# Squares of the second norm added on VectorE, silus and sigmoids of the token mixing in pairs

## The chip, the core and the metric

The kernel runs on one core of one Trainium2 chip. The metric is the device time of one execution in microseconds (us). The engines of the core work side by side, each through its own list of instructions: TensorE (PE, matrix products; PEld is its weight load), VectorE (DVE), ScalarE (ACT), GpSimdE (POOL), and SyncE (SP), which only starts transfers here. They wait for one another on semaphores, counters that an instruction raises when it is done.

## What is computed

Two blocks of a language model in fp32, for one sequence of 256 tokens with 1024 channels. Only what bears on the change stands here:

```python
def reference(x, ...):
    x = first_block(x, ...)      # short convolution and gated delta rule, w_o, then a feed-forward net
    return second_block(x, ...)

def first_block(x, ...):
    ...
    x = x + conv_ffn(rmsnorm(x, norm_ffn_g), w_up, ffn_conv_w, w_down)
    return rmsnorm(x, norm_final_g)

def second_block(x, ...):
    xn = rmsnorm_2(x, norm1_g)
    qa, ka, va, qr, kr, vr, gr, gate_a, gate_b = [xn @ part for part in w_in]
    qa, ka = rmsnorm_2(qa per head, q_norm_g), rmsnorm_2(ka per head, k_norm_g)
    o_a = dilated attention of qa, ka, va
    o_r = head_groupnorm(retention(qr, kr, vr), ret_gn_g, ret_gn_b) * silu(gr)
    y = sigmoid(gate_a) * (o_a @ w_proj_a) + sigmoid(gate_b) * (o_r @ w_proj_b)
    x = x + y @ w_out
    return x + square(relu(rmsnorm_2(x, norm2_g) @ w_up)) @ w_down
```

The "second norm" of the title (norm 2 in the code, counted from 0) is the final norm of the first block and the first of the second block taken together: it needs two sums of squares over the channels, one of x and one of x times the gain `norm_final_g`.

## The kernel before

**Blocks.** All weights are cut into 177 blocks of 1 MB (16 tiles of 128 x 128). `plan()` lists them; a block has a kind and a number, as ("qa", 0), and `AT` gives its place n. TensorE goes through them in `stream(n)`. To keep fp32 accuracy with a faster matrix format, each factor is split in a high and a low part, and a tile product is three matmuls: high x high, high x low, low x high, 48 to a block. Activations stand transposed, channels on the partitions and the 256 tokens along them; a block mostly makes two channel tiles, a 128 x 512 result.

**The path of a weight block.** SyncE loads block n + 3 into one of four buffers (`raw`) once TensorE is done with block n - 1. ScalarE makes the high part `wh` (`split`, L898) and VectorE the low part `wl` = raw - wh (L1225, 128 x 2048). In step n each engine does the split of block n + 3, then what `schedule()` puts into `TODO[n]` with `put(n, step, ...)`, in the order of the puts. VectorE first evicts the result of block n out of PSUM (`take(n)`, times the norm's factor `rb`), then splits, then does its steps. Exceptions stand in tables: for n in `AHEAD` VectorE splits block n + 3 before the norm and the eviction; `LOW_LATE` and `HIGH_LATE` put the split behind the steps. TensorE has two PSUM banks for these results (psS0, psS1), so block n can begin once block n - 2 is evicted. What TODO[n - 1] gives TensorE is strewn into its stream of block n: a lone norm 2 after 5 of 16 tiles, a lone step after 8, two steps after 5 and 10.

**The second norm.** The last blocks of the first net are d1 8 to d1 10; behind them come qa 0, qa 1 and so on. `res2(j)` (VectorE, ScalarE) adds the residual to pair j of the channel tiles, for j = 0 to 3, and makes its high and low parts (Yh, Yl), which qa 0 reads. In `sum2(j)` ScalarE squares the pair into `sq` and, with the gain, into `t2` (two buffers each), and GpSimdE adds them onto `ss0` and `ss1` (`add_squares(2, j)`, `tt` at L1631). Tile pair 3 has the buffers of pair 1, so ScalarE's `squares` waits until the adds of pair 1 are done. `norm(2)`: TensorE sums ss0 and ss1 over the partitions (L577), ScalarE and VectorE make from it `rfin` and `rb`, and VectorE can evict qa 0. For each pair of heads `sqh` squares the evicted queries: ScalarE makes the high part of the square (Zh), GpSimdE the whole square `sq` and then the low part Zl = sq - Zh; in the next block TensorE sums both (`colsum2`, L624 and L625), and ScalarE and VectorE finish the head's norm (`rmsh`).

**The stretch gr to tb.** Blocks gr 0 to gr 7 are the retention's gate, ta 0 to 3 and tb 0 to 3 the two gates of the mixing. VectorE evicts each to `y[n % 2]`. ScalarE takes it from there through silu (`silur`, L986) or sigmoid (`sig`, L974). The next eviction to the same y has to wait for that:

```python
if before in SIG:                       # before = SEQ[n - 2]
    dve.wait_ge(sem["sg"], SIG[before] + 1)
if before and before[0] in ("z", "gr"):
    dve.wait_ge(sem["zs" if before[0] == "z" else "sr"], before[1] + 1)
tt(y[n % 2][:], ps, two(rb[:]), ALU.mult, "ev")
```

Beside these blocks runs the group norm of the retention, from gr 3 to tb 0, one piece i a step: `ret_o(i)` (TensorE's product, L850; VectorE's bn_stats, bn_aggr and, once ScalarE has made the inverse deviation with Ln and Exp at L1165 and L1167, the scaled result `acc`, L1563), `ret_t(i - 1)` (TensorE transposes it, L860; ScalarE scales it, L1175; GpSimdE multiplies by silu(gr)) and `ret_x(i - 2)` (high part L901 and low part). ScalarE holds one table of functions at a time: silu, sigmoid, and Ln with Exp each need another one, and ACT_TABLE_LOAD fetches it. Copy and Square work with each.

Of the kernel before, what the change touches and what calls it, by code (L numbers as in the profile page):

```python
# [16 lines left out]
ALU = mybir.AluOpType  # L17
# [49 lines left out]
AT = {key: n for n, key in enumerate(SEQ)}  # L67
# [60 lines left out]
def schedule():  # L128
# [3 lines left out]
    def put(n, step, *a):  # L132
        todo[n].append((step, a))
# [4 lines left out]
    for i, kind in enumerate("kqv"):  # L138
        for j in range(4):
            n = AT[(kind, j)]  # L140
# [12 lines left out]
    for h in range(0, H1, 2):  # L153
        n = 10 + h // 2
# [22 lines left out]
    for j in range(4):  # L177
        n = AT[("x", j)]
# [3 lines left out]
        n = AT[("gb", j)]  # L182
        put(n + 1, "sig", "gb", j)
    for j in range(4):
        n = AT[("z", j)]
# [5 lines left out]
    for j in range(FF1):  # L191
        n = AT[("u1", j)]
# [4 lines left out]
    for step, q, j in (("res2", 0, 8), ("sum2", 0, 8), ("res2", 1, 9), ("res2", 2, 10), ("wl", AT[("d1", 9)] + 3, 10),  # L197
                       ("sum2", 1, 10), ("sum2", 2, 10), ("res2", 3, 10), ("sum2", 3, 10)):
        put(AT[("d1", j)], step, q)
# [3 lines left out]
    for kind in ("qa", "ka"):  # L203
        for j in range(6):
            n = AT[(kind, j)]
# [4 lines left out]
    n = AT[("kr", 0)]  # L210
# [7 lines left out]
    n = AT[("vr", 2)]  # L218
    for h in range(RH):
        put(n + h, "ret_s", h)  # L220
    for i in range(8):
        put(AT[("gr", i)] + 1, "silur", i)
    n = AT[("gr", 3)]
# [7 lines left out]
    for kind in ("ta", "tb"):  # L231
        for j in range(4):
            put(AT[(kind, j)], "sig", kind, j)
    put(AT[("pa", 1)], "ma")
# [9 lines left out]


TODO = schedule()

LASTS = (AT[("wo", 3)], AT[("d1", 10)], AT[("w2", 3)])
AHEAD = {n + 1 for n in LASTS}

# [33 lines left out]
def program(nc, wts, par_d, x_d, abw_d, sums_d, mask_d, sel_d, md_d, dr_d, out_d):  # L284
    with ExitStack() as ctx:
# [3 lines left out]
        sem = {name: ctx.enter_context(nc.semaphore("s_" + name)) for name in SEMS}  # L289
# [586 lines left out]
        def _(act):  # L876
# [323 lines left out]
            for n in range(-1, NB):  # L1200
# [14 lines left out]
                for step, a in TODO[n]:  # L1215
                    if step in steps:
                        steps[step](*a)
# [5 lines left out]
        def _(dve):  # L1223
# [269 lines left out]
            def res2(j):  # L1493
# [5 lines left out]
                gained(Yl, Yh, lambda k: gg[:, k:k + 1], "xbh", "xb", j)  # L1499

            def res3(j):
                complete("w2", j)
                tt(pair(xT, j), psA[j][:], pair(xT, j), ALU.add, "r3")
                gained(Xl, Xh, lambda k: pcol("g_n2", k), "x3h", "x3", j)
# [81 lines left out]
            def res4(q):  # L1586
# [5 lines left out]
                     "rows": rows, "kk": kk, "tok": tok, "level": level, "state": state, "wstate": wstate,  # L1592
                     "onorm": onorm, "mixc": mixc, "mix": mix, "res1": res1, "res2": res2, "res3": res3, "x2": x2,
                     "rtok": rtok_, "rmsh": rmsh, "att_s": att_s_, "att_o": att_o, "ret_s": ret_s, "ret_o": ret_o,
# [34 lines left out]
        def _(pool):  # L1629
            def tt(out, a, b, op, name):  # L1630
                pool.tensor_tensor(out, a, b, op).then_inc(sem[name], 1)  # L1631
# [99 lines left out]
            def add_squares(i, j):  # L1731
                base = {1: 0, 2: 2, 3: 7}[i]
                per = 2 if i == 2 else 1
                done = {1: 0, 2: 4, 3: 12}[i]
                if j == 0:
                    return
                for g in range(per):
                    pool.wait_ge(sem["sqr"], done + per * j + g + 1)
                    src = (sq, t2)[g][j % 2][:]
                    last = j == 3 and g == per - 1  # L1740
                    name = "ss" if last else "ssa"
                    if j > 1:
                        pool.wait_ge(sem["ssa"], base + per * (j - 2) + g + 1)
                    tt(ss[g][:], ss[g][:], src, ALU.add, name)

# [12 lines left out]
            def ffn2(j):  # L1758
# [5 lines left out]
                     "lev0": lev0, "level": level, "state": state, "osq": osq, "sqh": sqh, "zg": zg, "mix": mix,  # L1764
                     "res1": lambda j: add_squares(1, j), "sum2": lambda j: add_squares(2, j),
                     "res3": lambda j: add_squares(3, j), "ret_t": ret_t,
# [97 lines left out]
```

## Time and profile before

| | us |
|---|---|
| median of 3 runs | 1154.15 |
| lowest, highest run | 1153.98, 1157.34 |
| the profiled execution | 1158.51 |
| its span, first to last instruction | 1156.7 |
| busy in the span: TensorE | 1137.4 |
| VectorE | 768.6 |
| ScalarE | 603.4 |
| GpSimdE | 206.2 |
| mean granted clock of TensorE, share of full | 0.997 |

The profile is a record of one execution. Times in it count from the start of the span. In a timeline a row is one instruction or several alike, and the bracket tells how long its engine had been idle and whose work ended that; with no bracket the engine had been busy. Instructions follow one another before the one ahead has wholly ended, so that two of 0.69 us may take 1.29 us together. Tile names are without buffer numbers: psS is psS0 or psS1, and mix or gdn are memory regions that hold many tiles in turn.

### The profile page before, as it was taken

The numbers are of one execution on the slowest core, as the hardware profiler recorded it, in microseconds if no ns is written. First come the engines' busy times: TensorE is split into PE (matmuls) and PEld (weight loads), VectorE is DVE, ScalarE is ACT, GpSimd is POOL, SyncE is SP. The second block draws the span as 40 slices with busy tenths as digits, with TensorE's granted clock in tenths as the row PEclk, the third lists the DMA queues.
The fourth block names the chain that finished last, engine by engine and source line by source line (L and its number), as shares of the span: only waits on it lengthen the run. The fifth ranks groups of instructions, "written<-read, shape, count | busy, mean of one in ns | idle before, by whom it ended". The sixth has DMA issues, their size and how long they took to land. (4 is left out here: it accounts for less than half of the span.)

```text
span 1156.7 us, 23245 instructions
## 1 busy us (share of the span) xinstructions
PE 1137.4 (98%) x10262; PEld 1103.4 (95%) x10262; DVE 768.6 (66%) x875; ACT 603.4 (52%) x692; POOL 206.2 (18%) x129
## 2 busy tenths in 40 slices
PE   8999999999999999999899999999999999999998
PEld 7978899999999999999899999999999999999998
DVE  7999775435456897796768757645666556756453
ACT  6978342242664765565655534433798335544341
POOL 0442353210133200000445400000011002211010
PEclk9999999999999999999999999999999999999999
DMA  8443332333365555655555553445445555556552
GB/s 306 149 142 127 137 111 80 106 110 132 124 222 202 194 185 187 208 190 187 178 178 168 169 187 133 146 146 182 146 146 166 191 190 182 183 187 206 191 187 105
DMA packets 27748, 192.81 MB, mean 167 GB/s; under 512 B 3072, under 2 KB 3200, under 8 KB 4992
## 3 DMA queue, kind: packets, MB, share of 16 engines
q1 hardware_dynamic: 27648, 191.33, 48.9%
q8 instruction: 81, 1.33, 0.5%
q14 instruction: 19, 0.16, 0.0%
HBM read 190.27 MB, written 1.05 MB: 165 GB/s over the span
## 5 line engine op out<-in xcount | busy, mean ns | idle before, releaser
L1225 DVE TENSOR_TENSOR wl<-raw,wh 128x2048 fp32r<-128x2048 f32 (+1 forms) x178 | 421.3, 2369 | 134.9 <-ACT wh L898 134.0
L898 ACT ACTIVATE wh<-raw 128x2048 fp32r<-128x2048 f32 x176 | 336.5, 1913 | 248.3 <-DMA raw<-in_wts 248.0
L563 PE MATMUL psS<-Yh,wh 128*128 128x256 f32 x1056 | 300.3, 284 | 1.4 <-issue 1.1
L563 PE MATMUL psS<-Yl,wh 128*128 128x256 f32 x1056 | 293.4, 278 | 0.0
L563 PE MATMUL psS<-Yh,wl 128*128 128x256 f32 x1056 | 293.4, 278 | 0.0
L563 PE MATMUL psS<-Xh,wh 128*128 128x256 f32 x896 | 260.7, 291 | 4.8 <-issue 3.2
L563 PE MATMUL psS<-Xl,wh 128*128 128x256 f32 x896 | 249.7, 279 | 0.0
L563 PE MATMUL psS<-Xh,wl 128*128 128x256 f32 x896 | 249.7, 279 | 0.0
L563 PEld LDWEIGHTS psS<-Yh,wh 128*128 128x128 f32 x1056 | 199.1, 189 | 4.5 <-issue 3.4
L563 PEld LDWEIGHTS psS<-Yl,wh 128*128 128x128 f32 x1056 | 198.9, 188 | 2.5 <-issue 1.9
L563 PEld LDWEIGHTS psS<-Yh,wl 128*128 128x128 f32 x1056 | 198.4, 188 | 0.0
L563 PEld LDWEIGHTS psS<-Xh,wh 128*128 128x128 f32 x896 | 168.7, 188 | 15.4 <-issue 11.0
L563 PEld LDWEIGHTS psS<-Xl,wh 128*128 128x128 f32 x896 | 169.6, 189 | 3.2 <-issue 3.2
L563 PEld LDWEIGHTS psS<-Xh,wl 128*128 128x128 f32 x896 | 169.0, 189 | 0.0
L1231 DVE SCALAR_TENSOR_TENSOR acc<-y,par,acc 128x254 f32<-128x254 f32 (+1 forms) x176 | 79.8, 517 | 8.1 <-ACT acc L946 8.1
L1225 DVE TENSOR_TENSOR y<-psS,rb 128x512 f32<-128x512 f32 x66 | 45.4, 688 | 47.8 <-PE psS L563 44.1
L1631 POOL TENSOR_TENSOR t<-t,mix 128x512 f32<-128x512 f32 x12 | 15.7, 1309 | 290.2 <-ACT t L1175 224.0
L551 PE MATMUL psS<-wh,Yh 128*128 128x256 f32 x224 | 63.4, 283 | 0.0
L551 PE MATMUL psS<-wh,Yl 128*128 128x256 f32 x224 | 62.4, 278 | 0.0
L551 PE MATMUL psS<-wl,Yh 128*128 128x256 f32 x224 | 62.3, 278 | 0.0
L1631 POOL TENSOR_TENSOR ss<-ss,sq 128x512 f32<-128x512 f32 x9 | 17.8, 1975 | 212.4 <-ACT sq L1099 212.4
L563 PE MATMUL psP<-Yh,wh 128*128 128x256 f32 x192 | 53.3, 278 | 0.0
(246 smaller groups left out, 2004.6 us busy)
## 6 DMA issues: line engine op xcount, KB each, us to landing
raw<-in_wts SPq DMA_DIRECT2D x176, 1024.0 KB, 4.9
raw<-in_wts SPq DMA_DIRECT2D x2, 512.0 KB, 5.8
gdn<-in_x SPq DMA_DIRECT2D x1, 1024.0 KB, 8.2
out<-head SPq DMA_DIRECT2D x4, 256.0 KB, 2.1
head<-in_x SPq DMA_DIRECT2D x1, 516.0 KB, 4.0
head<-in_x SPq DMA_DIRECT2D x1, 512.0 KB, 5.9
head<-in_sel SPq DMA_DIRECT2D x1, 512.0 KB, 4.8
xf<-in_dr SPq DMA_DIRECT2D x1, 512.0 KB, 5.6
```

The source lines that it names most:

```text
L551: mm = pe.matmul(o, a[:, kk_, t * P:(t + 1) * P], b, start=(p == 0 and t == 0 and i == 0), stop=(p == 14 and i == 2), skip_group_check=True)
L563: mm = pe.matmul(bank[:, half], a[:, n % SLOTS, p, :], b[:, kk_, :], start=(first and i == 0), stop=(last and i == 2), skip_group_check=True)
L898: act.activation(wh[:, n % SLOTS], raw[:, n % SLOTS], ACT.Copy).then_inc(sem["wh"], 1)
L1225: return dve.tensor_tensor(out, a, b, op)
L1231: dve.scalar_tensor_tensor(out=out, in0=a, scalar=s, in1=b, op0=op0, op1=op1).then_inc(sem[name], 1)
L1631: pool.tensor_tensor(out, a, b, op).then_inc(sem[name], 1)
```

## The change

The edits fall in two groups.

At the second norm: the adds of squares (`sum2`) go from GpSimdE to VectorE; for that, `res2(3)` stands before them in the schedule, and ScalarE keeps its old order by an exception (it squares pairs 1 and 2 before `res2(3)`). And qa 0 leaves `AHEAD`, so VectorE splits qa 3 after the eviction of qa 0 rather than before the norm.

In the stretch gr to tb: `silur` of two tiles stands in the step after the odd one, and `sig` of two ta tiles in the step of the odd one. The tb tiles stay as they were. TensorE's list of instructions is the same as before.

```diff
@@ schedule()
     for step, q, j in (("res2", 0, 8), ("sum2", 0, 8), ("res2", 1, 9), ("res2", 2, 10), ("wl", AT[("d1", 9)] + 3, 10),
-                       ("sum2", 1, 10), ("sum2", 2, 10), ("res2", 3, 10), ("sum2", 3, 10)):
+                       ("res2", 3, 10), ("sum2", 1, 10), ("sum2", 2, 10), ("sum2", 3, 10)):
...
     for i in range(8):
-        put(AT[("gr", i)] + 1, "silur", i)
+        put(AT[("gr", i | 1)] + 1, "silur", i)
...
         for j in range(4):
-            put(AT[(kind, j)], "sig", kind, j)
+            put(AT[(kind, j | 1 if kind == "ta" else j)], "sig", kind, j)
...
-AHEAD = {n + 1 for n in LASTS}
+AHEAD = {LASTS[0] + 1, LASTS[2] + 1}
@@ ScalarE
                 for step, a in TODO[n]:
-                    if step in steps:
+                    if step == "res2" and a == (3,):
+                        sum2(1)
+                        sum2(2)
+                    if step in steps and (step, a) not in (("sum2", (1,)), ("sum2", (2,))):
                         steps[step](*a)
@@ VectorE
+            def sum2(j):
+                if j == 0:
+                    return
+                for g in range(2):
+                    dve.wait_ge(sem["sqr"], 4 + 2 * j + g + 1)
+                    if j > 1:
+                        dve.wait_ge(sem["ssa"], 2 + 2 * (j - 2) + g + 1)
+                    tt(ss[g][:], ss[g][:], (sq, t2)[g][j % 2][:], ALU.add, "ss" if j == 3 and g else "ssa")
@@ GpSimdE
-                     "res1": lambda j: add_squares(1, j), "sum2": lambda j: add_squares(2, j),
+                     "res1": lambda j: add_squares(1, j),
```

VectorE around the second norm, before: the residual of pair 3, its low halves, the low parts of blocks qa 2 and qa 3, the norm, the evictions of qa 0 and qa 1, and the low part of qa 4.

```order
L1225 TENSOR_TENSOR head<-psP1,head 128x512 [waits s_mm]
L1231 SCALAR_TENSOR_TENSOR Yl<-head,small,Yh 128x256 [waits s_xbh] x2
L1225 TENSOR_TENSOR wl<-raw,wh 128x2048 [waits s_wh] x2
L1225 TENSOR_TENSOR lnt<-psP2,rfin 128x256 [waits s_nl]
L1225 TENSOR_TENSOR lnt<-lnt,rfin 128x256 [waits s_ms0]
L1225 TENSOR_TENSOR rb<-lnt,rfin 128x256 [waits s_nl]
L1225 TENSOR_TENSOR mix2<-psS0,rb 128x512 [waits s_rb,s_mm]
L1225 TENSOR_TENSOR mix2<-psS1,rb 128x512 [waits s_mm]
L1225 TENSOR_TENSOR wl<-raw,wh 128x2048 [waits s_wh]
```

After:

```order
L1228 TENSOR_TENSOR ss0<-ss0,sq1 128x512 [waits s_sqr]
L1228 TENSOR_TENSOR ss1<-ss1,t21 128x512 [waits s_sqr]
L1228 TENSOR_TENSOR ss0<-ss0,sq0 128x512 [waits s_ssa,s_sqr]
L1228 TENSOR_TENSOR ss1<-ss1,t20 128x512 [waits s_ssa,s_sqr]
L1228 TENSOR_TENSOR ss0<-ss0,sq1 128x512 [waits s_ssa,s_sqr]
L1228 TENSOR_TENSOR ss1<-ss1,t21 128x512 [waits s_ssa,s_sqr]
L1228 TENSOR_TENSOR wl<-raw,wh 128x2048 [waits s_wh]
L1228 TENSOR_TENSOR lnt<-psP2,rfin 128x256 [waits s_nl]
L1228 TENSOR_TENSOR lnt<-lnt,rfin 128x256 [waits s_ms0]
L1228 TENSOR_TENSOR rb<-lnt,rfin 128x256 [waits s_nl]
L1228 TENSOR_TENSOR mix2<-psS0,rb 128x512 [waits s_rb,s_mm]
L1228 TENSOR_TENSOR wl<-raw,wh 128x2048 [waits s_wh]
```

The six adds now stand between the low halves and the first wl, and of the two wl ahead of the norm the second now stands between the two evictions (mix2<-psS0 and mix2<-psS1).

ScalarE in the stretch, before: the steps of gr 5 and, from the second wh on, the start of gr 6. Each begins with the split (wh<-raw); mix2<-y is a silu, rsd the statistics, t20 and t21 the transposed result.

```order
L898 ACTIVATE wh<-raw 128x2048 [waits s_mm,s_raw3]
L986 ACT_TABLE_LOAD
L986 ACTIVATE mix2<-y1 128x512 [waits s_ev]
L882 ACT_TABLE_LOAD
L1165 ACTIVATE rsd<-bag,par 128x1 [waits s_bag]
L1167 ACTIVATE rsd<-rsd 128x1 [waits s_rl]
L901 ACTIVATE Zh<-t20 128x4x128 [waits s_rg]
L1175 ACTIVATE t21<-psP0,par 128x128 [waits s_qk,s_rtT]
L1175 ACTIVATE t21<-psP0,par 128x128 x3
L898 ACTIVATE wh<-raw 128x2048 [waits s_mm,s_raw0]
```

After, the steps of gr 5 and the start of gr 6:

```order
L898 ACTIVATE wh<-raw 128x2048 [waits s_mm,s_raw3]
L1165 ACTIVATE rsd<-bag,par 128x1 [waits s_bag]
L1167 ACTIVATE rsd<-rsd 128x1 [waits s_rl]
L901 ACTIVATE Zh<-t20 128x4x128 [waits s_rg]
L1175 ACTIVATE t21<-psP0,par 128x128 [waits s_qk,s_rtT]
L1175 ACTIVATE t21<-psP0,par 128x128 x3
L898 ACTIVATE wh<-raw 128x2048 [waits s_mm,s_raw0]
L986 ACT_TABLE_LOAD
L986 ACTIVATE mix2<-y1 128x512 [waits s_ev]
L986 ACTIVATE mix2<-y0 128x512 [waits s_ev]
L882 ACT_TABLE_LOAD
```

In gr 5 both table loads and the silu are gone, and gr 6 has two silus between two loads; the second of them is the one that stood at this place before, the first (of gr 4) is new in this step. VectorE's list in this stretch is unchanged: an eviction, a wl, the statistics.

## Rows read from the trace of the kernel before

**Rows 1.** The page, part 1: engines, busy us (share of the span) xinstructions
```profile
PE 1137.4 (98%) x10262; PEld 1103.4 (95%) x10262; DVE 768.6 (66%) x875; ACT 603.4 (52%) x692; POOL 206.2 (18%) x129
```

**Rows 2.** Timeline, TensorE: start us, us, operation, [idle before <-releaser]
```profile
574.73 3.52 PE L577 MATMUL psP<-ss,par 128*128 128x256 f32 x8 [3.02 <-POOL ss L1631]
...
582.48 0.36 PE L563 MATMUL psS<-Yh,wh 128*128 128x256 f32 x1 [0.46 <-issue]
...
585.12 0.48 PE L624 MATMUL psP<-Zh,onesr 128*128 128x512 f32 x1 [0.68 <-POOL Zl L1631]
...
878.01 0.66 PE L860 MATMUL psP<-par,acc 128*128 128x128 f32 x4 [0.54 <-DVE acc L1563]
...
887.52 0.36 PE L563 MATMUL psS<-Yh,wh 128*128 128x256 f32 x1 [0.68 <-issue]
```

**Rows 3.** Windows of TensorE: stretch, us, busy (x), granted clock, DMA share, GB/s
```profile
574.60:577.90 3.30, 3.17 (x9) 0.51 0.00 0
```

**Rows 4.** Timeline, GpSimdE, 571 to 592
```profile
571.36 3.31 POOL L1631 TENSOR_TENSOR ss<-ss,t 128x512 f32<-128x512 f32 x1
582.45 1.04 POOL L1631 TENSOR_TENSOR sq<-mix 128x512 f32<-128x512 f32 x1 [7.78 <-DVE mix L1225]
583.57 1.29 POOL L1631 TENSOR_TENSOR Zl<-sq,Zh 128x512 fp32r<-128x512 f32 x1
...
591.20 3.02 POOL L1631 TENSOR_TENSOR sq<-mix 128x512 f32<-128x512 f32 x1 [1.99 <-DVE mix L1225]
```

**Rows 5.** Groups of instructions by form, VectorE, whole span: busy us, mean ns
```profile
L1225 DVE TENSOR_TENSOR ss<-ss,sq 128x512 f32<-128x512 f32 x1 | 0.7, 693 | 0.0
```

**Rows 6.** Timeline, VectorE, 559 to 592
```profile
559.17 0.89 DVE L1231 SCALAR_TENSOR_TENSOR Yl<-head,small,Yh 128x256 fp32r<-128x256 f32 x2 [0.58 <-ACT Yh L901]
...
566.04 2.95 DVE L1231 SCALAR_TENSOR_TENSOR Yl<-head,small,Yh 128x256 fp32r<-128x256 f32 x2 [0.58 <-ACT Yh L901]
570.58 6.24 DVE L1225 TENSOR_TENSOR wl<-raw,wh 128x2048 fp32r<-128x2048 f32 x2 [1.58 <-ACT wh L898]
...
581.68 1.29 DVE L1225 TENSOR_TENSOR mix<-psS,rb 128x512 f32<-128x512 f32 x2
584.88 3.13 DVE L1225 TENSOR_TENSOR wl<-raw,wh 128x2048 fp32r<-128x2048 f32 x1 [1.91 <-ACT wh L898]
...
591.04 2.28 DVE L1225 TENSOR_TENSOR wl<-raw,wh 128x2048 fp32r<-128x2048 f32 x1
```

**Rows 7.** Timeline, ScalarE, around the second norm
```profile
567.30 0.63 ACT L1099 ACTIVATE sq<-head 128x512 f32<-128x512 f32 x1 [0.89 <-POOL ss L1631]
...
578.28 0.47 ACT L922 ACTIVATE lnt<-psP,par 128x256 f32<-128x256 f32 x1 [4.64 <-PE psP L577]
```

**Rows 8.** Timeline, ScalarE, from gr 4 to ta 1
```profile
821.74 1.91 ACT L898 ACTIVATE wh<-raw 128x2048 fp32r<-128x2048 f32 x1
...
830.10 1.93 ACT L898 ACTIVATE wh<-raw 128x2048 fp32r<-128x2048 f32 x1
...
837.62 1.92 ACT L898 ACTIVATE wh<-raw 128x2048 fp32r<-128x2048 f32 x1
839.56 1.28 ACT L986 ACT_TABLE_LOAD   x1
840.85 0.63 ACT L986 ACTIVATE mix<-y 128x512 f32<-128x512 f32 x1
...
842.80 0.29 ACT L1165 ACTIVATE rsd<-bag,par 128x1 f32<-128x1 f32 x1
...
852.64 1.92 ACT L898 ACTIVATE wh<-raw 128x2048 fp32r<-128x2048 f32 x1
...
862.12 1.90 ACT L898 ACTIVATE wh<-raw 128x2048 fp32r<-128x2048 f32 x1
...
871.50 1.90 ACT L898 ACTIVATE wh<-raw 128x2048 fp32r<-128x2048 f32 x1
```

**Rows 9.** Timeline, VectorE, in gr 6
```profile
839.58 2.29 DVE L1225 TENSOR_TENSOR wl<-raw,wh 128x2048 fp32r<-128x2048 f32 x1 [1.17 <-ACT wh L898]
```

More of the change, by code:

```diff
@@ L1592, in _ @@
                      "rows": rows, "kk": kk, "tok": tok, "level": level, "state": state, "wstate": wstate,
-                     "onorm": onorm, "mixc": mixc, "mix": mix, "res1": res1, "res2": res2, "res3": res3, "x2": x2,
+                     "onorm": onorm, "mixc": mixc, "mix": mix, "res1": res1, "res2": res2, "sum2": sum2, "res3": res3, "x2": x2,
                      "rtok": rtok_, "rmsh": rmsh, "att_s": att_s_, "att_o": att_o, "ret_s": ret_s, "ret_o": ret_o,
@@ L1731, in add_squares @@
             def add_squares(i, j):
-                base = {1: 0, 2: 2, 3: 7}[i]
-                per = 2 if i == 2 else 1
-                done = {1: 0, 2: 4, 3: 12}[i]
+                base = {1: 0, 3: 7}[i]
                 if j == 0:
                     return
[L1737 to L1744, printed above, removed]
+                pool.wait_ge(sem["sqr"], {1: 0, 3: 12}[i] + j + 1)
+                if j > 1:
+                    pool.wait_ge(sem["ssa"], base + j - 1)
+                tt(ss[0][:], ss[0][:], sq[j % 2][:], ALU.add, "ss" if j == 3 else "ssa")
             def ret_t(i):
```

## Prediction

> **What bounds the kernel now.** I read the page first: TensorE is busy for 98% of the span [rows 1]. So only its idle time and its clock can give anything back, and anything that makes it wait shows in full. The next view is TensorE's own timeline near the two places that the change touches. At the second norm it stands still for 3.02 us until GpSimdE's last add of squares is done, then computes the column sums in 3.52 us, waits 0.46 us for the eviction of qa 0, and 0.68 us for GpSimdE's low half of the first squares [rows 2]. In the stretch gr to tb it waits twice, 0.54 us for a ret_t and 0.68 us for an eviction [rows 2]. That is 5.4 us in all, 0.5% of the span. The third view is the clock: while those column sums ran, the granted clock was 0.51 of full [rows 3], the lower level of 1.2 GHz, and what TensorE had done before it fell was to idle for the 3.0 us of that wait. At full clock the sums take 3.52 / 2 = 1.76 us; with the slow first matmul behind them the low clock cost some 1.65 us.
>
> A measurement of this kernel can tell about 0.3% (3.5 us) from no change, which is the bound for "same" below.
>
> **Place one: the adds move to VectorE.** Before, the last of GpSimdE's six adds starts at 571.36 and takes 3.31 us, because VectorE holds a memory port with a weight subtraction (wl) just then; alone such an add takes 1.3 us [rows 4]. VectorE does one in 0.69 us [rows 5]. In the changed order they stand behind the low halves of the last residual tile. Those began at 566.04 and took 2.95 us beside GpSimdE; without it a pair takes 0.89 us, as at 559.17, so the adds start at 566.9 [rows 6]. Issued 0.6 us apart (two evictions take 1.29 us together [rows 6]), the two of tile 1 are done at 568.1. ScalarE's squares of tile 3 wait for these; they began at 567.30 [rows 7], so ScalarE runs 0.85 us later from here. The squares are done at 569.6 and the last add at 570.6. TensorE comes to the column sums at 574.73 - 3.02 = 571.7 (571.5, as the late low halves no longer hold it): the wait of 3.0 us goes, with 0.9 us to spare, and the low clock with it.
>
> What is late next. The logarithm behind the sums started at 578.28 after ScalarE had stood ready for 4.64 us, since 573.64 [rows 7]; now ScalarE is ready at 574.5 and the sums at 573.3, so it starts at 574.5. From its start to the end of the eviction of qa 0 it was 582.37 - 578.28 = 4.09 us [rows 6, 7]; that end, call it T, comes at 578.6. TensorE needed 582.02 - 574.73 = 7.3 us from the sums to the end of qa 1, 5.65 us at full clock, so it is there at 577.15 and waits 1.55 us where it waited 0.46. Up to here the change has gained 3.75 us.
>
> Now the part that the title of the change does not name: qa 0 leaves AHEAD, so VectorE's wl for qa 3 stands behind the eviction of qa 0 and in front of that of qa 1. Before, VectorE was busy with an eviction out of PSUM when GpSimdE squared the first tile (582.45, 1.04 us) and subtracted its high half (583.57, 1.29 us) [rows 4]. Now VectorE starts a wl at T - 0.1 us, just before GpSimdE's square. Exactly this pair stands at 591: wl starts at 591.04, the square at 591.20 takes 3.02 us [rows 4, 6]. So the square ends at T + 3.1. VectorE finishes the wl at T + 2.2, evicts qa 1 till T + 2.8, and asks for the next wl, whose high half is ready (584.88 is T + 2.5 in the old order [rows 6]), 0.3 us before the square ends. When both wait, they take turns: at 570.58 VectorE waited with a wl for GpSimdE's add, had the port at its end, and the next add, already started at 571.36, ended only 3.3 us later [rows 4, 6]. So the wl runs till T + 5.25 and the subtraction ends at T + 6.4. TensorE starts its norm matmul 0.26 us after such an end (583.57 + 1.29 against 585.12), at T + 6.66 = 585.3. It started at 585.12 before. The whole gain of 3.75 us is given back in a wait of 4.6 us where there was one of 0.7. Such an idle time is longer than the one after which the clock fell before; I take 1.4 us for a low clock behind it (0 and 1.7 are the ends). **Place one: +0.2 + 1.4 = +1.6 us.** For the later tiles TensorE comes to the head norm long after GpSimdE is done (before, its list of waits has one such wait, that of 0.68 us), so only the first counts.
>
> The Trainium skill ("SBUF — State Buffer", on the shared port pair) says that an operation of VectorE with two SBUF inputs and one of GpSimdE that reads SBUF lock each other out whole. The rows agree, and it says nothing of turns among operations that queue; by first-come alone the time is the same here, as the wl asks first.
>
> **Place two: silus and sigmoids in pairs.** ScalarE saves table loads: 6 to 4 for silu, 8 to 5 back to exp, 3 to 2 for sigmoid, six at 1.28 us = 7.7 us. Is that time on a path? One step of ScalarE in gr 6: split at 837.62, load, silu (done 841.48), load, and at 842.80 the statistics' logarithm [rows 8]. In the same time VectorE does its wl from 839.58 for 2.29 us, and ScalarE's logarithm comes 0.93 us after its end [rows 8, 9]. Both ways end at 5.2 us after the split. So without loads the step is not shorter: VectorE's chain takes it, and a step without silu stays at 7.5 us (837.62 to 852.64 is two).
>
> With a pair it becomes longer. The eviction of a tile waits until the silu of the tile two before it, which shares its buffer, is done. Before, that silu was a step earlier; now the even one of each pair is in the same step, behind the split and the load: 1.92 + 1.30 + 0.63 = 3.9 us after the split's start. Then VectorE evicts (0.6 us before the next can start), does its wl till 6.8, and the logarithm comes at 7.7; the rest of the step takes 2.33 us as before: 10.0 us instead of 7.5. Queued behind that eviction on VectorE are the wl and the bn_stats, for which ScalarE waits. Step by step against [rows 8]: gr 4 (no high half in it) 9.5 against 830.10 - 821.74 = 8.4, +1.1; gr 5 0; gr 6 +2.5; gr 7 0; ta 0 (silu pair, its sigmoid gone) 10.0 against 862.12 - 852.64 = 9.5, +0.5; ta 1 (two sigmoids, one load, 7.5 + 1.3 + 1.2) 10.0 against 9.4, +0.6. So the last y of the retention, for which ret_t waits at 878.01, comes 1.1 + 2.5 + 0.5 + 0.6 = 4.7 us later; I take 4.6. TensorE waited there already [rows 2], so all of it shows, some of it as waits for evictions in ta 2 and tb 0. The wait of 0.68 us at 887.52 goes. **Place two: 4.6 - 0.7 = +3.9 us**, and 1.4 us for the clock behind an idle time of about 3.4 us (ends 0 and 1.7): **+5.3 us.**
>
> The Trainium skill ("ScalarE: Activation LUTs", What ACT_TABLE_LOAD costs) gives 2.66 us for a switch, a load with a drain. Here the silu starts 0.01 us after a load of 1.28 us and the load 0.02 us after the split [rows 8]. By its figure six switches would be an estimated 16 us of ScalarE and would speak for the third rival below; but a step of the old order, with two switches, could not be 7.5 us then, and the rows decide.
>
> **Sum.** +1.6 + 5.3 = +6.9 us. The profiled execution took 1158.51 us (1156.7 us span, 1.8 around it), so it would be 1165.4 us; the median of the runs, 1154.15, is 4.4 us lower, some of which may be low clock that those runs did not have. The same step on the median gives 1161.0 us.
>
> **Rivals.**
> First, one collision only: GpSimdE's subtraction gets the port before the second wl, as a margin of 0.3 us decides it. It ends at T + 4.5, TensorE goes on at 583.35, 1.8 us earlier than before, with perhaps 0.8 us of low clock: -1.0 + 5.3 = +4.3 us, 1158.5 us. For it speaks the margin, against it the turns at 571. With no collision at all place one is -3.7 and the sum +1.6 us, 1155.8 us.
> Second, place two is absorbed: if the eviction with its silu still comes before TensorE and the norm chain need it, the step stays at 7.5 us, place two is 0 to -1.2 and the sum about +0.4 to +1.6 us, 1154.5 to 1156. Against it: ScalarE and VectorE have no slack left at 878.
> Third, the other side: faster. ScalarE's own queue sets the step, and each load taken away shortens the chain to ret_t, so that both waits of place two go (-1.2), and the port does not collide in place one (-3.7, and the low clock may have been absent in the timed runs): -4.9 us, 1149.2 us. It decides at the logarithm at 842.80: if that waited for ScalarE's queue alone and not for VectorE, this is what happens; there it has no idle time before it, which is for this rival, but VectorE's chain ends in the same tenth.
> That the change does not do what it says is excluded: VectorE has the six adds, ScalarE the pairs.
>
> **How the numbers follow.** Forecast 0.53; one collision 0.17; none 0.08; place two absorbed 0.10; faster 0.07; the rest (other sizes of both) 0.05, mostly within 0.3%. Slower by over 0.3%, above 1157.6 us: 0.53 + 0.17 + 0.06 of the edges = 0.76. Faster, below 1150.7 us: 0.07. Same: 0.17. The range goes from 1156, which takes in the one collision and most of none, to 1164: the forecast with 1.7 us at both low clocks, and with timed runs of before that had no low clock at the norm (1161.0 + 0.6 + 1.6, with some room).
>
> **What would show it.** Right: no idle time before the column sums, their 8 matmuls in 1.8 us; the first wl behind the eviction of qa 0; the first square on GpSimdE 3.0 us and its subtraction over 3 us; TensorE idle for some 4.6 us before the first head norm. In gr 4, gr 6 and ta 0, VectorE's eviction released by ScalarE's silu and steps of 9.5 to 10 us; TensorE idle for about 3 us before the last ret_t. Wrong: a subtraction of 1.4 us (first rival), evictions in gr released by TensorE (second), or the last ret_t earlier than before relative to the start of gr (third).

## The result: slower by 0.7%

| | before | after |
|---|---|---|
| median of 5 runs beside each other, us | 1157.34 | 1165.11 |
| lowest, highest | 1153.98, 1160.77 | 1164.59, 1166.40 |
| the profiled execution | 1158.51 | 1166.11 |
| its span | 1156.7 | 1164.3 |
| mean granted clock | 0.997 | 0.993 |

The ratio is 1.0070 with a 95% interval of 1.0041 to 1.0099. The direction was forecast, and so was the size between the two profiled executions: +7.6 us against +6.9. The time itself, forecast as 1161.0 with a range of 1156 to 1164, came out 1.1 us above the range. Three of the five runs of before are those that the prediction started from; the other two took 1160.06 and 1160.77 us. The ratios here and below come from all the runs and are not exactly the quotients of the medians.

**The page and TensorE's waits.** Part 1 of the page of after, to be held against [rows 1]:

```profile
PE 1139.6 (98%) x10262; PEld 1106.5 (95%) x10262; DVE 765.4 (66%) x881; ACT 595.6 (51%) x686; POOL 198.7 (17%) x123
```

Six adds moved from GpSimdE (129 to 123 instructions) to VectorE (875 to 881), and ScalarE lost six table loads, 7.8 us of busy time (603.4 to 595.6). GpSimdE and ScalarE both have less to do, and the kernel is slower. Two rows of what TensorE waited for in after, the first two that name a releaser (engine line, tile, releaser: us in total, times, longest us):

```profile
PE psP L624 <- POOL Zl L1643: 4.6, 1, 4.6
PE psP L860 <- DVE acc L1575: 3.0, 1, 3.0
```

**Place one.** TensorE's timeline of after, around the second norm, answers to the first three of [rows 2]:

```profile
572.85 1.89 PE L577 MATMUL psP<-ss,par 128*128 128x256 f32 x8
...
580.44 0.36 PE L563 MATMUL psS<-Yh,wh 128*128 128x256 f32 x1 [1.95 <-issue]
...
586.96 0.77 PE L624 MATMUL psP<-Zh,onesr 128*128 128x512 f32 x1 [4.56 <-POOL Zl L1643]
```

No wait before the column sums, and 1.89 us for them instead of 3.52. Then 1.95 us where 0.46 stood (the eviction of qa 0), and 4.56 where 0.68 stood. GpSimdE's and VectorE's timelines of after show why; they answer to [rows 4] and [rows 6]:

```profile
580.42 3.02 POOL L1643 TENSOR_TENSOR sq<-mix 128x512 f32<-128x512 f32 x1 [189.69 <-DVE mix L1228]
583.51 3.19 POOL L1643 TENSOR_TENSOR Zl<-sq,Zh 128x512 fp32r<-128x512 f32 x1
```

```profile
571.59 0.68 DVE L1228 TENSOR_TENSOR ss<-ss,t 128x512 f32<-128x512 f32 x1
...
579.65 0.69 DVE L1228 TENSOR_TENSOR mix<-psS,rb 128x512 f32<-128x512 f32 x1
580.26 2.28 DVE L1228 TENSOR_TENSOR wl<-raw,wh 128x2048 fp32r<-128x2048 f32 x1
582.46 0.68 DVE L1228 TENSOR_TENSOR mix<-psS,rb 128x512 f32<-128x512 f32 x1
583.06 2.52 DVE L1228 TENSOR_TENSOR wl<-raw,wh 128x2048 fp32r<-128x2048 f32 x1
```

The adds are done at 572.27, before TensorE asks at 572.85. Then the two engines take turns: the subtraction wl starts at 580.26, GpSimdE's square at 580.42 and is held to 583.44 instead of lasting 1.04 us; the next wl, started at 583.06, is held until then and a bit (2.52 instead of 2.28), and GpSimdE's own subtraction behind it takes 3.19 instead of 1.29. The head norm waits for that.

**The clock behind that wait.** Windows of after: stretch, us, then busy us and instructions of TensorE, its weight loads, VectorE, ScalarE and GpSimdE, then the granted clock, DMA share and GB/s:

```profile
586.00:587.00 1.00, 0.04 (x1) 0.07 (x1) 0.00 (x0) 0.00 (x0) 1.00 (x2) 0.53 0.00 0
587.00:596.00 9.00, 9.00 (x38) 8.57 (x39) 1.04 (x3) 3.64 (x4) 2.10 (x2) 0.50 0.01 2
596.00:598.00 2.00, 2.00 (x19) 2.00 (x18) 1.54 (x2) 0.00 (x0) 0.77 (x1) 0.93 0.46 78
```

The clock fell to its lower level, 1.2 GHz, at 586.1, late in the 4.56 us of idle time, and stayed there until 596.3, though TensorE had been computing without a gap since 586.96: it lasted 10.2 us in all. From this head norm to the next one it is 599.02 - 586.96 = 12.06 us in after and 593.05 - 585.12 = 7.93 in before: 4.1 us lost where the forecast had 1.4.

**Place two.** ScalarE's timeline of after from gr 4 to ta 2, which answers to [rows 8]; the seven wh are the splits, one at the start of each step, and mark off six steps:

```profile
827.69 1.90 ACT L898 ACTIVATE wh<-raw 128x2048 fp32r<-128x2048 f32 x1
829.61 1.28 ACT L986 ACT_TABLE_LOAD   x1
830.91 1.16 ACT L986 ACTIVATE mix<-y 128x512 f32<-128x512 f32 x2
...
837.20 1.92 ACT L898 ACTIVATE wh<-raw 128x2048 fp32r<-128x2048 f32 x1
...
844.63 1.93 ACT L898 ACTIVATE wh<-raw 128x2048 fp32r<-128x2048 f32 x1
...
854.68 1.92 ACT L898 ACTIVATE wh<-raw 128x2048 fp32r<-128x2048 f32 x1
...
862.11 1.92 ACT L898 ACTIVATE wh<-raw 128x2048 fp32r<-128x2048 f32 x1
...
872.15 1.93 ACT L898 ACTIVATE wh<-raw 128x2048 fp32r<-128x2048 f32 x1
...
882.08 1.90 ACT L898 ACTIVATE wh<-raw 128x2048 fp32r<-128x2048 f32 x1
```

The steps of gr 4 to gr 7, ta 0 and ta 1 are 9.5, 7.4, 10.05, 7.4, 10.0 and 9.9 us; 9.5, 7.5, 10.0, 7.5, 10.0 and 10.0 were forecast. VectorE's evictions in gr 4, gr 6 and ta 0 of after are the held instructions:

```profile
831.64 0.69 DVE L1228 TENSOR_TENSOR y<-psS,rb 128x512 f32<-128x512 f32 x1 [3.01 <-ACT mix L986]
...
848.61 0.69 DVE L1228 TENSOR_TENSOR y<-psS,rb 128x512 f32<-128x512 f32 x1 [4.33 <-ACT mix L986]
...
866.08 0.69 DVE L1228 TENSOR_TENSOR y<-psS,rb 128x512 f32<-128x512 f32 x1 [4.32 <-PE psS L563]
```

The last row names TensorE, and the prediction had said ScalarE. But this eviction too starts 0.74 us behind the start of its pair of silus (865.34), as the other two do (830.91 and 847.87), and TensorE had by then computed the next block as well. The eviction of ta 2 (881.76) stands 0.74 us behind the pair of sigmoids of ta 0 and ta 1 (881.02).

And TensorE pays in three places, behind the evictions of ta 0 and ta 2 and before the last ret_t, with no wait of 0.68 us at tb 2 any more:

```profile
866.87 0.36 PE L563 MATMUL psS<-Yh,wh 128*128 128x256 f32 x1 [0.89 <-issue]
...
882.55 0.36 PE L563 MATMUL psS<-Yh,wh 128*128 128x256 f32 x1 [0.83 <-issue]
...
888.59 0.66 PE L860 MATMUL psP<-par,acc 128*128 128x128 f32 x4 [2.97 <-DVE acc L1575]
```

That is 4.7 us of waits, where before had 0.54. The last ret_t starts 888.59 - 878.01 = 10.6 us later than before, of which 6.0 were there at the second head norm (599.02 - 593.05): 4.6 us are from here, as forecast. Behind the last of them the clock was at 1.2 GHz for 3.4 us and cost 1.7.

**What neither kernel's code explains.** At full granted clock TensorE's matmuls of 256 columns follow each other at one of two distances, 0.113 or 0.118 us. Windows of TensorE alone in the same stretch, before first, then after (stretch, us, busy and instructions, granted clock, DMA share, GB/s; an instruction of 0.28 us that reaches over an edge is counted too, some 3 for each stretch):

```profile
920.00:940.00 20.00, 20.00 (x172) 1.00 0.50 167
940.00:960.00 20.00, 20.00 (x172) 1.00 0.60 205
```

```profile
920.00:940.00 20.00, 20.00 (x179) 1.00 0.58 184
940.00:960.00 20.00, 20.00 (x179) 1.00 0.52 188
```

From 888 to 985 the before profile ran at the slow distance, and from 894 on the after profile at the fast one. Measured between the same matmuls, after was 12.2 us behind when before stood at 884, and 7.6 at 987; less the wait of 0.7 us that only before has in between, the distance gave 3.9 us back. The same thing made after late ahead of the change: at 344 us both have one longer distance, of 0.130 us in before and of 0.154 in after, and then before goes over to the fast distance while after stays at the slow one until its column sums at 392 (340 to 380 us holds 354 matmuls in before and 342 in after, both at a granted clock of 1.00). That is an offset of 1.7 us that was there at 400 us and still at 561, in code that is the same in both. Elsewhere both alternate, and every change of distance falls on an interruption of the stream or just behind one (a helper's matmuls, a wait, or a single longer distance as at 344). The sum over the whole profile is then: 1.7 us of offset; 6.0 - 1.7 = 4.2 in place one; +4.6 and -0.7 in place two, +1.7 for its clock; -3.9 from the distance: the 7.6 us.

### The profile page after: what moved, and what is told of

Same layout as the page of the kernel before. It is cut to its first block and busy times, and to the rows that moved or that the text cites. A ratio compares the mean times of both kernels' runs of the same rounds, so it can differ in the third digit from the quotient of the medians.

```text
span 1164.3 us, 23239 instructions
## 1 busy us (share of the span) xinstructions
PE 1139.6 (98%) x10262; PEld 1106.5 (95%) x10262; DVE 765.4 (66%) x881; ACT 595.6 (51%) x686; POOL 198.7 (17%) x123
## 5 line engine op out<-in xcount | busy, mean ns | idle before, releaser
L563 PEld LDWEIGHTS psS<-Yl,wh 128*128 128x128 f32 x1056 | 201.5, 191 | 2.6 <-issue 1.9
L563 PEld LDWEIGHTS psS<-Xh,wh 128*128 128x128 f32 x896 | 168.8, 188 | 14.3 <-issue 10.6
L1643 POOL TENSOR_TENSOR sq<-mix 128x512 f32<-128x512 f32 x12 | 26.3, 2195 | 203.1 <-DVE mix L1228 203.0
L563 PE MATMUL psP<-Zh,wh 128*128 128x256 f32 x192 | 53.0, 276 | 0.0
```

What stands on the lines that cost most here:

```text
L563: mm = pe.matmul(bank[:, half], a[:, n % SLOTS, p, :], b[:, kk_, :], start=(first and i == 0), stop=(last and i == 2), skip_group_check=True)
```

## The experiments

The theory has three parts: the gain of the moved adds is real (T1); it is given back because qa 0 left AHEAD, so that wl and GpSimdE's first square and subtraction meet (T2); the pairing costs time where a silu that an eviction waits for has moved into the eviction's own step (T3). The rivals: VectorE's adds themselves make the norm late (R1); place two is paid by anything that pairs (R2); the low clock is free (R3).

**Only place one.** After, with silus and sigmoids one by one again:

```diff
-        put(AT[("gr", i | 1)] + 1, "silur", i)
+        put(AT[("gr", i)] + 1, "silur", i)
-            put(AT[(kind, j | 1 if kind == "ta" else j)], "sig", kind, j)
+            put(AT[(kind, j)], "sig", kind, j)
```

> The changed kernel with silus and sigmoids as before: place one alone. Theory (VectorE's wl between the two evictions locks GpSimdE out twice): no wait at the column sums, 4.6 us of idle time before the first head norm, the low clock behind it, and from the start of that head norm on as late as in the changed kernel, about +4 us against before with the low clock; in gr to tb the two waits of 0.5 and 0.7 us of before. Rival (all of the loss is in the gr stretch, the moved adds gain 3 to 5 us): 3 to 5 us faster than before.

1160.79 us, ratio 1.0036 (1.0009 to 1.0063). TensorE of this kernel at the head norm:

```profile
585.95 0.76 PE L624 MATMUL psP<-Zh,onesr 128*128 128x512 f32 x1 [3.62 <-POOL Zl L1643]
```

The wait is shorter than in after (4.56) only because TensorE was late for it: its clock fell already at 580.2, 0.8 us behind the end of the wait of 2.07 us before qa 2 (579.43), and for 10.2 us again. GpSimdE's two instructions take the same 3.02 and 3.19 us. Place one alone makes the kernel slower. In the profile the +4 us are not there: at the second head norm this kernel is 595.93 - 593.05 = 2.9 us late, of which 0.7 were there ahead of the change, so 2.2 us, because this low clock fell partly on time in which TensorE was idle anyway. The median is 4.1 us above that of before; which low clock the other runs had, no trace shows.

**Place one with qa 0 back in AHEAD.** The kernel above with one more line:

```diff
-AHEAD = {LASTS[0] + 1, LASTS[2] + 1}
+AHEAD = {n + 1 for n in LASTS}
```

> As e1, but block qa 0 is back in AHEAD, so the wl of qa 3 stands before the norm again; the adds stay on VectorE. Theory: GpSimdE's first square takes 1.0 us and its subtraction 1.3 us again, the wait before the first head norm is 0.7 us, the one before qa 2 up to 2 us; no low clock around it. The start of the head norm comes 3.3 us earlier than before plus 1.6 us of low clock in its profile: 1.7 to 3.5 us faster than before. Rival (the adds on VectorE are what costs, whatever stands between the evictions): as slow as e1.

1155.86 us, ratio 0.9975 (0.9953 to 0.9996). TensorE and GpSimdE of this kernel:

```profile
574.32 1.89 PE L577 MATMUL psP<-ss,par 128*128 128x256 f32 x8
...
582.34 0.36 PE L563 MATMUL psS<-Yh,wh 128*128 128x256 f32 x1 [2.38 <-issue]
...
584.98 0.47 PE L624 MATMUL psP<-Zh,onesr 128*128 128x512 f32 x1 [0.69 <-POOL Zl L1643]
```

```profile
582.32 1.04 POOL L1643 TENSOR_TENSOR sq<-mix 128x512 f32<-128x512 f32 x1 [189.85 <-DVE mix L1228]
583.44 1.28 POOL L1643 TENSOR_TENSOR Zl<-sq,Zh 128x512 fp32r<-128x512 f32 x1
```

One line of the schedule turns a loss of 0.36% into a gain: the medians of the two kernels are 4.9 us apart and the intervals do not meet. How large the gain over before is stays less sure, 0.25% by the ratio, which just excludes no change, and 0.8 us by the medians. In its profile the head norm comes 3.3 us earlier than in before, counted from the 3.2 us that it was late ahead of the change. The collision is gone (1.04 and 1.28 us), the adds stay on VectorE and the column sums still do not wait. R1 falls; T1 and T2 hold.

**Only AHEAD.** Before, with qa 0 taken out of AHEAD and nothing else (the line above the other way round).

> Before, with only qa 0 taken out of AHEAD: the adds of squares are still on GpSimdE. Theory: the wait of 3.0 us at the column sums stays and the wait of 3.6 to 4.7 us before the first head norm is there as well, GpSimdE's square 3.0 us and its subtraction 3.2 us; place one costs 4 us and more against before. Rival (the late wl is harmful only together with the adds on VectorE): 0.7 us before the head norm.

```profile
576.51 2.77 PE L577 MATMUL psP<-ss,par 128*128 128x256 f32 x8 [3.01 <-POOL ss L1631]
...
590.02 0.77 PE L624 MATMUL psP<-Zh,onesr 128*128 128x512 f32 x1 [4.42 <-POOL Zl L1631]
```

TensorE's rows of this kernel have both waits, 3.01 us for the adds, which GpSimdE still makes, and 4.42 us for the subtraction, and a low clock at each. GpSimdE's square and subtraction are as long as in after:

```profile
583.48 3.02 POOL L1631 TENSOR_TENSOR sq<-mix 128x512 f32<-128x512 f32 x1 [7.03 <-DVE mix L1225]
586.57 3.19 POOL L1631 TENSOR_TENSOR Zl<-sq,Zh 128x512 fp32r<-128x512 f32 x1
```

So the collision needs the order alone, and not the moved adds. The time, 1161.59 us, is that of one run.

**The first square on ScalarE.** After, with the `sq` of the first pair of heads made by ScalarE, so that GpSimdE has only the subtraction to do there:

```diff
+                if i == 12:
+                    act.activation(sq[0][:], pair(QK[kind], j), ACT.Square).then_inc(sem["sqp"], 1)
...
+                if i > 12:
+                    tt(sq[i % 2][:], pair(QK[kind], j), pair(QK[kind], j), ALU.mult, "sqp")
```

> The changed kernel, but ScalarE makes the whole square of the first query tile too (one more Square of 0.6 us), so that GpSimdE has only the subtraction there and one meeting with VectorE. Theory (each operation of GpSimdE that meets a wl costs the length of that wl): the subtraction starts about 1.3 us after the eviction's end under the first wl, which ends at 2.2, and is over at 3.4 to 3.5 us; TensorE waits 1.6 us instead of 4.6 before the first head norm, too short for a fall of the clock; the head norm comes 3 us earlier. Rival (what is late is VectorE or ScalarE, and not GpSimdE): the wait stays at 4 us or more.

```profile
581.11 1.92 POOL L1645 TENSOR_TENSOR Zl<-sq,Zh 128x512 fp32r<-128x512 f32 x1 [190.86 <-ACT sq L1133]
```

GpSimdE subtracts once behind one wl, 1.92 us, not behind two; TensorE waited 1.48 us for it instead of 4.56, and its clock did not fall there. From the column sums to the head norm it took 583.29 - 572.09 = 11.2 us against 14.1 in after. That is place one repaired by another way than the schedule, which speaks for the port and against anything that the line of AHEAD may do besides. The one run's time, 1168.32 us, says nothing of it: this execution kept the slow distance of matmuls from 870 to its last ones at 1163.

**The clock kept busy.** After, with 36 matmuls that nobody reads, placed where TensorE would wait for the head norm:

```diff
+                    for _ in range(36):
+                        pe.matmul(psA[2][:, 0], onesr[:], Yh[:, 0], start=True, stop=True)
```

> The changed kernel with 36 extra matmuls of TensorE (4.1 us at full clock, into a bank that nobody reads) in the place where it waits for the first head norm. They add work that nothing needs. Theory (the idle time itself makes the clock fall, and the low clock of 10.2 us in the changed kernel's profile costs 4 us): the head norm starts as late as before, after at most 0.6 us of idle time, no low clock from there on; in the profile 4 us less than the changed kernel from the head norm to the end. Rival (the low clock comes from somewhere else): it falls all the same.

TensorE of this kernel:

```profile
587.58 0.50 PE L624 MATMUL psP<-Zh,onesr 128*128 128x512 f32 x1 [0.20 <-POOL Zl L1645]
...
595.54 0.39 PE L624 MATMUL psP<-Zh,onesr 128*128 128x512 f32 x1
```

The head norm comes no earlier, but the way to the next one takes 7.96 us instead of 12.06: what the low clock cost in place one is 4.1 us, now by a run of its own, and R3 falls. The median, 1162.94 us, is 2.2 us under that of after, but the ratio to before, 1.0051 (1.0021 to 1.0081), has an interval that overlaps that of after (1.0041 to 1.0099), so the runs alone do not show the gain. Nor does the profiled run's span, 1164.5, as it ran at the slow distance from 888 to 994.

**Only place two.** Before, with the pairs:

```diff
-        put(AT[("gr", i)] + 1, "silur", i)
+        put(AT[("gr", i | 1)] + 1, "silur", i)
-            put(AT[(kind, j)], "sig", kind, j)
+            put(AT[(kind, j | 1 if kind == "ta" else j)], "sig", kind, j)
```

> Before, with silus and sigmoids in pairs: place two alone. Theory (evictions held by the paired silu): ScalarE's steps of gr 4, gr 6 and ta 0 take 9.5 to 10 us, gr 5 and gr 7 7.4 us; waits of TensorE of 0.9, 0.8 and 3.0 us in ta 2, tb 0 and before the last ret_t; that ret_t 4.6 to 4.8 us later than before, about +4 us against before, more with a low clock. Rival (saved table loads are worth their time): faster by 1.2 us, no idle time of TensorE in the stretch.

1160.59 us, ratio 1.0027 (1.0001 to 1.0052). TensorE waits in the same three places as in after, 0.89, 0.83 and 2.98 us:

```profile
881.99 1.12 PE L860 MATMUL psP<-par,acc 128*128 128x128 f32 x4 [2.98 <-DVE acc L1563]
```

Place two stands by itself: 0.27% here and 0.36% for place one alone make 0.63%, and after has 0.70%.

**Only the silus in pairs** (the first of those two lines).

> Before, with only the silus in pairs; the sigmoids of ta one by one. Theory: steps of 9.5 to 10 us of ScalarE in gr 4 and gr 6, 11.5 to 12 in ta 0 (silu pair and a sigmoid), and TensorE waits before the last two ret_t, 1.6 and 4.0 us: about 6 us in all against 1.2 us before. So the silus carry all of the loss and the pairs of sigmoids give 1 to 2 us back. Rival (both kinds of pairs cost alike): half of the loss of the paired kernel, some 2 us.

One run, 1160.31 us. TensorE waited 0.88 us at 859.7, 1.39 and 3.94 us before two ret_t, and a low clock came with the last. So the silus are the harm; the sigmoid pairs do not add to it but take a little of it away (6.2 us of waits without them, 4.7 with them).

**Only the sigmoids of ta in pairs** (the second line).

> The kernel before with one edit: the sigmoids of ta 0 and ta 1 (and ta 2 and ta 3) are made together. My theory: TensorE's waits in the stretch gr to tb, 0.54 and 0.68 us before, are at most 0.3 us together; everything ahead of it as before (3.0 us at the column sums). Rival (any pairing lengthens the chain): a wait of 1 us or more before the last ret_t.

One run, 1158.23 us. TensorE has no idle time from 855 to 890, where before had 0.54 and 0.68. The pair of sigmoids does hold VectorE once, at the eviction of ta 2:

```profile
870.89 0.69 DVE L1225 TENSOR_TENSOR y<-psS,rb 128x512 f32<-128x512 f32 x1 [2.52 <-ACT mix L974]
```

But the next eviction starts 7.3 us behind it (878.19), where before took 9.4, and TensorE waits for neither. R2 falls: this pair, too, delays an eviction, and it costs TensorE nothing. Only with the late silus ahead of it does TensorE wait behind the same eviction (0.83 us in after).

**The same pairs, the silus one step earlier.** Before, with the sigmoid pairs and:

```diff
-        put(AT[("gr", i)] + 1, "silur", i)
+        put(AT[("gr", i | 1)], "silur", i)
```

> As e3 with the same pairs and as many table loads, but each pair of silus stands one step earlier (in the step of the odd tile), so that no eviction waits for a silu of its own step. Theory: no step over 8 us in gr, VectorE's evictions released by TensorE, the last ret_t waits 0 to 0.5 us; 0.5 to 1.3 us faster than before. Rival (pairs as such, two silus or sigmoids in one step, make the chain longer): as slow as e3.

1154.64 us, ratio 0.9980 (0.9960 to 1.0001), an interval that just takes in no change. The pairs save eight loads here (684 instructions of ScalarE against 692), not six, and the even tile's silu is done before its buffer is wanted. VectorE's eviction in gr 4 of this kernel is released by TensorE and no longer by ScalarE:

```profile
825.91 0.69 DVE L1225 TENSOR_TENSOR y<-psS,rb 128x512 f32<-128x512 f32 x1 [0.42 <-PE psS L563]
```

TensorE has no idle time from gr to tb. Held against the kernel with only place two this is T3: the same pairs, one step's difference in the place of the silus, and medians 6.0 us apart, with the slowest of these ten runs (1156.89) faster than the fastest of those (1158.75). That it is also faster than before is likely and not shown.

**Both repairs.** After, with qa 0 in AHEAD and the silu pairs one step earlier (the two lines shown above):

> The changed kernel with two edits: qa 0 stays in AHEAD, and each pair of silus is issued one step earlier (with the odd tile's block instead of one behind it). My theory: the two gains seen apart add up, since they stand 270 us apart. Place one: no wait for the adds, 2.4 us before qa 2 and 0.7 us before the head norm instead of 3.0, 0.5 and 0.7, and no low clock there, -2.8 us. Place two: no wait of TensorE from gr to tb, -1.2 us. Together -4.0 us, a ratio of 0.9965 (0.993 to 0.999, because the pitch of the matmuls between two interruptions moves single runs by some us). Rival: the gain of one place is eaten by the other (ScalarE comes 0.85 us later from the norm on, so waits return in gr to tb): then those waits are 1 us or more and the ratio is 0.998 to 1.000.

1151.77 us (1150.13 to 1155.66, 11 runs; before beside it 1158.41, 22 runs), ratio 0.9937 (0.9913 to 0.9961): the lowest median of all kernels here, and an interval that excludes no change. Its TensorE around the norm:

```profile
571.66 1.89 PE L577 MATMUL psP<-ss,par 128*128 128x256 f32 x8
...
579.70 0.36 PE L563 MATMUL psS<-Yh,wh 128*128 128x256 f32 x1 [2.40 <-issue]
...
582.34 0.47 PE L624 MATMUL psP<-Zh,onesr 128*128 128x512 f32 x1 [0.63 <-POOL Zl L1643]
```

There is no idle time of TensorE from 855 to 890, and the granted clock is full until the last instruction. At the split of 560.07, where before has 559.44, the profile is 0.6 us late; at the head norm it is 585.12 - 582.34 = 2.8 us early: 3.4 us from place one, where 2.8 was expected. With the 1.2 us of place two the schedule accounts for 4.6 of the profile's 7.9 us (1156.7 to 1148.8). The rest is mostly the fast distance of matmuls, which this execution kept from 876 on.

**Qa 0 in AHEAD, silus one by one, sigmoids of ta in pairs.**

```diff
-        put(AT[("gr", i | 1)] + 1, "silur", i)
+        put(AT[("gr", i)] + 1, "silur", i)
-AHEAD = {LASTS[0] + 1, LASTS[2] + 1}
+AHEAD = {n + 1 for n in LASTS}
```

> The changed kernel with qa 0 kept in AHEAD, the silus one at a time as before, and only the sigmoids of ta for two tiles at a time. My theory: place one -2.8 us as with AHEAD alone; in gr and ta no eviction waits for a silu of its own step, so steps stay at 7.5 us, one load and its return are saved in ta, and the last ret_t's 0.5 us and the later eviction's 0.7 us of waiting go or stay within 0.3: -1 us. Together -3.8 us, a ratio of 0.9967 (0.993 to 0.999). Rival: any pairing lengthens the chain to ret_t, sigmoids too: then TensorE waits 1 us or more for ret_t and the ratio is 0.998 to 1.001.

1154.86 us (12 runs), ratio 0.9957 (0.9930 to 0.9983). TensorE's waits are those of the kernel with both repairs (2.41 and 0.69 us at the norm, none from 840 to 890). Its span is 3.1 us longer, 1151.9 against 1148.8, and it ran at the slow distance from 867 to 981 where the other ran at the fast one from 876 on. The other saves six more loads; with no wait left in gr to tb they can give nothing by the rows, and whether the 3.1 us between the medians too are only the distance is not shown.

## Why the prediction was right, and where it was not

**Right in place one, up to the head norm.** The adds hide on VectorE (done at 572.27, less the 1.7 us of offset 570.5; 570.6 was forecast). The eviction of qa 0 ends at 580.34, less 1.74 of offset 578.6, as forecast. TensorE waits 1.95 us for it (1.55 forecast). The two collisions on the port came in the forecast order, with 3.02 and 3.19 us, and the head norm at 586.96 - 1.74 = 585.2 against 585.3. The whole gain was given back, and the one-collision rival, which hung on a margin of 0.3 us, did not come: the second wl asked at 583.06 and GpSimdE's square ended at 583.44.

**Wrong in place one: the low clock behind it.** "I take 1.4 us for a low clock behind it (0 and 1.7 are the ends)". The upper end came from the one low clock behind a wait that the prediction had read in the trace of before, some 3.4 us long. At a wait of 4.6 us it was 10.2 us long in this trace, and 6.8 in the one with only AHEAD changed. The term measured 4.1 us, by the rows and by the kernel whose clock was kept busy. The upper end was no bound at all; it was the only case seen. Why this low clock lasted three times as long stays open.

**Right in place two.** The evictions behind the silus, the six step lengths, the last ret_t 4.6 us later (as forecast), the 0.68 us at tb 2 gone, the low clock (1.7, forecast 1.4, within its ends). The third rival, that each saved load shortens a chain, is refuted by the same rows: six loads fewer, and no step shorter by more than 0.1 us.

**Wrong in the anchor.** The step was put on the median of three runs, 1154.15 us. All five of before beside the changed kernel have a median of 1157.34, and the other comparisons 1156.64 (31 runs, 1153.64 to 1166.87) and 1158.41 (22 runs). The difference of the medians is 7.8 us; on 1157.34 the forecast step of 6.9 would have given 1164.2, and the measured step on 1154.15 would have given 1161.9, inside the range. So it is this term, 3.2 us too low, that took the time out of the range. The prediction put some of the 4.4 us between the profiled execution and that median down to low clock. Some of it may be: of the 64 other runs of before that count, the 20 with a mean clock of 0.996 have a median of 1159.5 us and the 22 with 0.999 one of 1156.4. But at 0.999 alone they reach from 1153.64 to 1166.11 us. What differs from run to run at the same clock may be the distance of the matmuls; only profiled executions could show it, so this is not shown.

So the sum of +6.9 met +7.6 partly by luck: 2.7 us too little for the low clock in place one and 1.7 us of offset ahead of the change stand against 3.9 us of faster matmuls behind it, and neither of the last two could be told from a row of before.

## What to carry to other kernels

When work is moved between VectorE and GpSimdE, list what each of them starts in the few microseconds after the moved work too: here the order of one subtraction, a line beside the real change, took back all that the change had gained and brought a low clock on top. Batching to save table loads cost time here where a buffer came free late because of the batch. Put the batch at the earliest step that its last member allows, and check who frees its buffers. And a wait on the engine that sets the time costs more than its length when the clock falls behind it, so price it with a wide upper end.

## What was not expected of the hardware

**Two distances of matmuls at one granted clock**, 0.113 and 0.118 us for 256 columns, each held over 100 us and more, with the granted clock at 1.00 in both (the windows above). One distance changes into the other at interruptions; which comes is not settled: the kernel with both repairs and the one with the sigmoids of ta in pairs leave TensorE equally free of waits in gr to tb, and one ran fast and one slow behind it. It moved the profile of after by 3.9 us in one stretch, and that of the kernel with the first square on ScalarE, slow from 870 to 1163, fell another 9.2 us behind after between 898 and 1131. The Trainium skill ("TensorE: Matmul & The Clock Gate", Back-to-back issue gap) gives columns / 2.4 + 2.5 ns at the higher clock for an isolated matmul, by which an estimated 109 ns for 256 columns, and for a sustained stream of weight loads and matmuls some 81 ns at 128 columns and 131 ns at 512. The two measured here lie above the first and between the latter two.

**The length of a low clock.** With idle times of 3.0 us it lasted 3.4 us in before (column sums), and did not come at all in the kernel with only the pairs (the sums took 1.99 us behind a wait of 3.01). With 3.9 us it lasted 3.4 in the kernel with only the silus in pairs, with 4.4 to 4.6 us it lasted 6.8 us in one kernel and 10.2 in another, and in the kernel with only place one it fell 0.8 us after a wait of 2.1 us had ended and lasted 10.2, across a second wait of 3.6 us. In five other kernels a wait of 2.1 to 2.4 us at that place brought no low clock. What decides whether it comes, and how long it lasts, stays open.
